# One stream of split weight pieces for the hybrid mixer, with the attention's steps placed between its products

## The chip, the cores and the metric

The kernel runs on one core of one Trainium2 chip. The metric is the device time of one execution in microseconds (us), the median of several runs; lower is better.

## What is computed

The reference is a pair of transformer blocks on 512 tokens of 1024 channels, all in f32. The change touches the middle part of the first block, the hybrid mixer, between two feed-forward parts (`ffn1`, `ffn2`):

```
h = h + 0.5 * rms_norm(swiglu(rms_norm(h, g1)), g2)          # ffn1
u = rms_norm(h, mix_pre_g)
gate_br, x_br, q, k, v, g_lru, g_attn = split(u @ w_in)       # widths 1024 1024 1024 256 256 1024 1024
xc = causal_depthwise_conv(x_br)                              # 4 taps
r, i = sigmoid(block_diag(xc, w_a)), sigmoid(block_diag(xc, w_x))
log_a = -8 * r * softplus(-lambda);  a = exp(log_a)
b = sqrt(max(-expm1(2 * log_a), 0)) * (i * xc)
y_lru = scan(a, b) * gelu(gate_br)                            # h[t] = a[t] h[t-1] + b[t]
y_attn = sliding_window_attention(rope(q), rope(k), v, sinks) # 16 heads of 64, 4 kv heads, window 128
m = (sigmoid(g_lru) * (y_lru @ w_proj_lru) + sigmoid(g_attn) * (y_attn @ w_proj_attn)) @ w_out
h = h + rms_norm(m, mix_post_g)
h = h + 0.5 * rms_norm(swiglu(rms_norm(h, g3)), g4)          # ffn2
```

The second block (an even mixer, a window attention with context, and two layers of a mixture of 32 experts) is not touched.

## The kernel before

Activations lie transposed: 128 channels on the partitions, 512 tokens along the row, eight such tiles (`KT` = 8) to 1024 channels. A weight matrix comes from HBM in chunks of 1 MB (two output tiles) into `slot0` and `slot1` in turn, issued by SyncE in `stream` (L409 to L417); a slot is loaded again once the second tile made from it is done (`full[1]`, `full[3]`).

**Split products.** Where precision allows TensorE's faster f32r form, a product is made of three: weight and activation are each cut into a high part (a copy rounded to f32r) and a low part (what is left). For each of the eight k, high weight x low activation and high x high; then eight times low weight x high activation: 24 matmuls of 512 columns for an output tile (`split_products`, L527 to L543). Half a slot, the weights of one output tile, is a *piece*. ScalarE makes the high part of a piece (`high`, L1089), another engine the low part: VectorE in the feed-forwards (`low`, L1477), GpSimd in the mixer (`low`, L2070). Semaphores `wh_ready`, `wl_ready` and `wh_used` order them. Elsewhere (`dense`, L525) a tile is eight plain f32 matmuls, each of which shows as two rows in the trace. Four PSUM banks take the tiles in turn, with `full[j]` and `free[j]`.

**Queues.** Every engine works through its own list strictly in order, written out by hand. Nothing is planned at run time.

**The junction** between two parts (`junction`, L1056 on ScalarE and L1479 on VectorE): per k, the last part's output is scaled by its norm factor and added to `lat`, and the sum times the gain is split; TensorE starts the next part's first tiles k by k. The norm factor `rs` itself comes later, from a sum of squares on TensorE, a square root on ScalarE (L1068) and a reciprocal on VectorE (L1470). In the feed-forwards three tiles are opened this way (`gate_up`), in the mixer two.

**The mixer** was a chain of stages:
- `xbr` and `q1`, 16 split tiles; VectorE scales each by `rs`, makes the normalised u1 (L1877) and the convolution (L1879, L1882).
- the LRU's block-diagonal products (L901, L902), per tile two f32 matmuls and two sigmoids on ScalarE (L1287, L1288), one behind the other.
- `kv1`, plain f32 on u1, with `partner` (L908, a matmul with a permutation for rope); Exp and Tanh on ScalarE (L1292, L1293); on VectorE, 1 - a^2 by way of a reciprocal (L1895 to L1900), and rope (L1642 to L1645).
- `gate`, plain f32; Sqrt and Gelu (L1307, L1310), scans (L1909), the gated product (L1914).
- a phase end: all engines wait for one another (L344).
- `attend`: 32 units (a pair of heads and 128 queries). Per unit: scores (L692), mask and maximum (L1608, L1614), exponentials (L1171), transposes (L710), their copies (L1182), products with the values (L727), normalisation (L1633), a turn (L735) and its copy (L1191). GpSimd copies the queries (L2026). Unit m's steps stand beside those of units m-1 to m-4. Then a second phase end.
- splits of u1, LRU output and attention output (L1921, L1923, L2118), then `merge`, 32 split tiles in rounds of four (gate, projection, gate, projection), with Sigmoid on ScalarE (L1332) and L1929 and L1931 on VectorE.
- `out1`, plain f32, with `output` (L1045, L1046) and the sum of squares (L638, L640).

The core of a split tile and of the merge order:

```python
for k in range(n):
    for part_of, flag in ((high, first and k == 0), (low, False)):
        mm = nc.tensor.matmul(out, piece[0][k], part_of[k], start=flag, stop=False)
mm.then_inc(wh_used, 1)
low_ready()
for k in range(n):
    mm = nc.tensor.matmul(out, piece[1][k], high[k], start=False, stop=(last and k == n - 1))
```

Of the kernel before, what the change touches and what calls it, by code (L numbers as in the profile page):

```python
# [50 lines left out]
MERGE_PIECES = 4 * KT  # L51

PIECES_BEFORE, _n = {}, 0
for _name, _pieces in ((1, FFN_PIECES), ("mixer", 2 * KT), ("merge", MERGE_PIECES), (2, FFN_PIECES), ("even_in", 2 * KT),
                       ("even_out", KT), ("qkv", KT + 4)):
    PIECES_BEFORE[_name] = _n
    _n += _pieces
# [17 lines left out]
DENSE = [("gu1", 22, 11), ("down1", 8, 2), ("xbr", 4, 2), ("q1", 4, 2), ("kv1", 2, 1),  # L75
         ("gate", 4, 2), ("merge", 16, 8), ("out1", 4, 2), ("gu2", 22, 11), ("down2", 8, 2),
# [37 lines left out]
def program(nc, d):  # L114
    ctx = ExitStack()
    with ctx:
# [10 lines left out]
        with ExitStack() as plain:  # L127
# [6 lines left out]
            big = shared("big", BIG)  # L134
        w_low = [sb(f"w_low{s}", [P, SLOT], F32R) for s in range(2)]
# [6 lines left out]
        sb("big_rest", [P, BIG - 2 * FT * S])  # L142
        cxt = cxt_s[:, :].rearrange("p (k t) -> p k t", k=KT)
# [9 lines left out]
        tabs = sb("tabs", [P, 4, S])  # L153
# [34 lines left out]
        xbr = part(0, [KT, XPAD])  # L188
        xc = part(KT * XPAD, [KT, S])
        o = KT * (XPAD + S)  # L190
        gr = part(o, [KT, S])
        gi = part(o + KT * S, [KT, S])
        qt1 = part(o + 2 * KT * S, [KT, S])
        kt1 = part(o + 3 * KT * S, [2, S])
        qk1 = part(o + 2 * KT * S, [KT + 2, S])
        v1 = part(o + 3 * KT * S + 2 * S, [LT, C])
# [7 lines left out]
        lru_low = split_view(KT * XPAD)  # L204
        u1_low, att_low = u_high, u_low
        u1_high, lru_high, att_high = split_view(0), split_view(o + KT * S), split_view(o + 2 * KT * S)

        p1_high = split_view(o + KT * S)
        p1_low = [flat[a // (FT * S)][:, a % (FT * S):a % (FT * S) + S] for a in
                  [o + k * S for k in range(5)] + [FT * S + k * S for k in range(2)] + [o + 3 * KT * S]]  # L210
        assert o + 5 * S <= FT * S and FT * S + 2 * S <= o + KT * S
        lru_w = ar_u[:, KT * S:KT * S + 2 * KT * P].rearrange("p (g k c) -> p g k c", g=2, k=KT)
        merged = gr
# [75 lines left out]
        bank = [ctx.enter_context(nc.psum_tensor(f"bank{i}", [P, 512], F32)) for i in range(8)]  # L289
# [219 lines left out]
        def _(pe):  # L509
# [45 lines left out]
            def gate_up(n, J):  # L555
# [5 lines left out]
                def piece(j):  # L561
                    s, at, ring = ffn_piece(j)
                    return tiles_of(hi_ring[ring], KT), tiles_of(w_low[s][:, at], KT)
# [1723 lines left out]
```

## Time and profile before

| | us |
|---|---|
| median of 3 runs | 3428.01 (3425.63 to 3429.47) |
| the profiled execution | 3430.5 |
| its span, first to last instruction | 3428.7 |
| TensorE matmul busy | 2938.1 (86%) |
| VectorE busy | 1341.5 (39%) |
| ScalarE busy | 794.0 (23%) |
| GpSimd busy | 513.7 (15%) |
| HBM traffic | 203 GB/s over the span |
| mean granted TensorE clock | 0.907 of full speed |

In the profile PE is TensorE's matmuls, PEld its weight loads, DVE VectorE, ACT ScalarE, POOL GpSimd, SP SyncE. A number like L811 is a line of the kernel. Matmul rows overlap, since their ends are modelled: the spacing of their starts is the rate. PEclk is the granted clock, 1.0 for 2.4 GHz and 0.5 for 1.2 GHz. The mixer lies between about 404 and 1025 us of the span.

### The profile page before, as it was taken

To read this page: it belongs to the slowest core of one execution; us is meant where nothing else is said; L and a number is where in the kernel's file an instruction comes from. 1 tells how busy PE (TensorE), PEld (TensorE's weight loads), DVE (VectorE), ACT (ScalarE), POOL (GpSimd) and SP (SyncE) were. 2 spreads that over 40 slices of the span, in tenths; PEclk is the share of its full clock that TensorE was granted. 3 is DMA by queue.
4 is the path that set the end of the run, shared out by engine and by line. 5 is a ranking of instruction groups with operands and counts; after the bars stand their busy time and mean duration, and the time that the engine had idled before them with its cause. 6 is when DMAs were issued, how large, how long until landed. Compare 5 with 4: busy or idle time off the path is not lost. (4 is left out here: it accounts for less than half of the span.)

```text
span 3428.7 us, 37322 instructions
## 1 busy us (share of the span) xinstructions
PE 2938.1 (86%) x12832; PEld 1906.0 (56%) x12832; DVE 1341.5 (39%) x2369; ACT 794.0 (23%) x1393; POOL 513.7 (15%) x604
## 2 busy tenths in 40 slices
PE   6999888898998999699876888887587986888886
PEld 4888664476856888477653333333365843333333
DVE  4776575664117675612231111111458822111112
ACT  3332323343313322222220000000325711000000
POOL 0111140005400011131301111111310000111110
PEclk9999999758999999899977999998698997999997
DMA  4666421101223566411026999999010024999997
GB/s 162 220 220 220 155 98 50 37 0 63 97 103 137 196 214 236 152 50 49 25 94 238 400 400 403 397 401 358 29 62 1 0 100 175 404 402 396 402 401 291
DMA packets 117463, 671.63 MB, mean 196 GB/s; under 512 B 16398, under 2 KB 20878, under 8 KB 51984
## 3 DMA queue, kind: packets, MB, share of 16 engines
q1 hardware_dynamic: 77456, 542.37, 40.6%
q0 software_dynamic: 33600, 104.90, 8.7%
q10 hardware_dynamic: 6336, 23.50, 1.8%
q8 instruction: 35, 0.57, 0.1%
q14 instruction: 36, 0.29, 0.0%
HBM read 672.52 MB, written 24.38 MB: 203 GB/s over the span
## 5 line engine op out<-in xcount | busy, mean ns | idle before, releaser
L811 PE MATMUL bank<-big 128*64 128x512 f32 x1040 | 482.8, 609 | 105.5 <-DMA big<-in_w 103.8
L814 PE MATMUL bank<-big 128*64 128x512 f32 x1040 | 485.0, 611 | 0.0
L1792 DVE TENSOR_TENSOR big<-big,bank 64x512 f32<-64x512 f32 x65 | 44.9, 692 | 919.0 <-ACT big L1229 919.0
L811 PEld LDWEIGHTS bank<-big 128*64 128x64 f32 x1040 | 139.0, 140 | 418.6 <-issue 416.5
L826 PE MATMUL bank<-big 128*64 128x512 f32 x1040 | 288.8, 707 | 44.4 <-DVE big L1796 44.4
L1524 DVE SCALAR_TENSOR_TENSOR tabs<-tabs,tmp 128x1024 f32<-128x1024 f32 x160 | 193.2, 1222 | 175.3 <-DMA tabs<-in_wm 174.4
L537 PE MATMUL bank<-act_low 128*128 128x512 f32 (+1 forms) x480 | 166.1, 363 | 47.9 <-POOL u_split L2081 25.5
L2096 POOL DMA_DIRECT2D tabs<-in_wm x160 | 84.8, 530 | 743.2 <-DVE tabs L1524 742.4
L826 PEld LDWEIGHTS bank<-big 128*64 128x64 f32 x1040 | 83.4, 160 | 201.1 <-issue 199.7
L537 PE MATMUL bank<-u_split,w_high 128*128 128x512 f32 x448 | 179.1, 400 | 8.2 <-ACT w_high L1089 8.2
L537 PE MATMUL bank<-act_high,w_high 128*128 128x512 f32 x438 | 175.7, 401 | 10.8 <-POOL u_split L2118 10.8
L537 PE MATMUL bank<-act_low,w_high 128*128 128x512 f32 x458 | 170.1, 396 | 9.5 <-POOL w_low L2070 8.4
L1089 ACT ACTIVATE w_high<-slot 128x1024 fp32r<-128x1024 f32 (+1 forms) x116 | 117.7, 1040 | 232.5 <-DMA slot<-in_w 123.2
L543 PE MATMUL bank<-u_split,w_low 128*128 128x512 f32 x656 | 162.2, 389 | 3.0 <-DVE w_low L1477 3.0
L1229 ACT ACTIVATE big<-bank 64x512 f32<-64x512 f32 x65 | 38.2, 588 | 537.5 <-PE bank L811 537.5
L537 PE MATMUL bank<-u_low,w_high 128*128 128x512 f32 x384 | 151.6, 395 | 0.0
L2070 POOL TENSOR_TENSOR w_low<-slot,w_high 128x1024 fp32r<-128x1024 f32 x48 | 117.3, 2447 | 221.5 <-ACT w_high L1089 221.5
L543 PE MATMUL bank<-act_high,w_low 128*128 128x512 f32 (+1 forms) x608 | 146.2, 382 | 0.0
L1235 ACT ACTIVATE big<-bank 128x512 f32<-128x512 f32 x65 | 38.8, 597 | 461.9 <-PE bank L826 461.9
L543 PEld LDWEIGHTS bank<-u_split,w_low 128*128 128x128 f32 x656 | 123.0, 188 | 29.3 <-DVE w_low L1477 3.8
L814 PEld LDWEIGHTS bank<-big 128*64 128x64 f32 x1040 | 138.8, 140 | 0.0
L543 PE MATMUL bank<-act_low,w_low 128*128 128x512 f32 (+1 forms) x592 | 135.5, 372 | 0.0
(339 smaller groups left out, 5408.4 us busy)
## 6 DMA issues: line engine op xcount, KB each, us to landing
big<-in_w SPq DMA_DIRECT2D x402, 1024.0 KB
slot<-in_w SPq DMA_DIRECT2D x100, 1024.0 KB, 4.8
tabs<-in_wm POOLq DMA_DIRECT2D x160, 512.0 KB, 4.8
slot<-in_wd SPq DMA_DIRECT2D x16, 1408.0 KB, 6.8
big<-yb ACTq DMA_DIRECT2D x20, 512.0 KB, 4.8
rows<-big ACTq DMA_DIRECT2D x10, 512.0 KB, 2.6
lat<-in_x SPq DMA_DIRECT2D x1, 2048.0 KB, 9.5
out<-lat SPq DMA_DIRECT2D x4, 512.0 KB, 3.2
```

Source lines behind the costliest of these rows:

```text
L537: mm = nc.tensor.matmul(out, piece[0][k], part_of[k], start=flag, stop=False)
L543: mm = nc.tensor.matmul(out, piece[1][k], high[k], start=False, stop=(last and k == n - 1))
L811: ga = nc.tensor.matmul(bank[0][lo, :], xT[:, 4 * c + k, :], wslot[c][:, k * EF:(k + 1) * EF], **flags)
L814: mm = nc.tensor.matmul(bank[0][hi, :], xT[:, 4 * c + k, :], wslot[2 + c][:, k * EF:(k + 1) * EF], **flags)
L826: mm = nc.tensor.matmul(bank[4][half, :], hT[:, 2 * c + k, :], wslot[4 + c][:, k * D + n * 512:k * D + (n + 1) * 512], start=(c == 0 and k ...
L1089: nc.scalar.activation(rings[ring][:, 0:at.stop - at.start], slot[s][:, at], ACT.Copy).then_inc(wh_ready, 1)
L1229: nc.scalar.activation(hsil[MB:2 * MB, :], bank[0][0:MB, :], ACT.Silu).then_inc(q["sg_ready"], 1)
L1235: nc.scalar.activation(ysb, bank[4][:, :], ACT.Copy).then_inc(q["y_ready"], 1)
L1524: nc.vector.scalar_tensor_tensor(mslot[m % 2], mslot[m % 2], 1.0, crow, ALU.mult, ALU.mult, accum_out=modf[:, idx:idx + 1]).then_inc(mod_d ...
L1792: nc.vector.tensor_tensor(hmul[MB:2 * MB, :], hsil[MB:2 * MB, :], bank[0][MB:2 * MB, :], ALU.mult).then_inc(q["h_ready"], 1)
L2070: nc.gpsimd.tensor_tensor(w_low[s][:, at], slot[s][:, at], rings[ring][:, 0:at.stop - at.start].bitcast(F32), ALU.subtract).then_inc(wl_re ...
L2096: pool.dma_start(mslot[m % 2], d["wm"][(MOD_OF[1] + MOD_OF[2])[m] // 2]).then_inc(mod_load[m % 2], 16)
```

## The change

The mixer becomes one stream of 68 pieces (34 chunks, the same weights in another order): tiles 0 to 7 x branch, 8 to 15 q, 16 and 17 k, 18 and 19 v (256 columns wide), 20 to 27 attention gate, 28 to 35 LRU gate (Gelu), 36 to 43 gate of the LRU projection, 44 to 51 LRU projection, 52 to 59 attention projection, 60 to 67 output. All 68 are split products. The phase ends inside the mixer are gone.

- All gates and projections of u use the unnormalised u split at the junction (`u_high`, `u_low`); the norm factor goes on the products (`scaled`), into the rope tables, and for the values, whose tokens lie on the partitions, into `rs_col`, made by four narrow matmuls. u1 and its split are gone.
- The opening is the feed-forwards': three tiles are opened k by k.
- The low halves of the weights are made by VectorE (`mixer_low`), none by GpSimd.
- The attention's 108 steps (36 x 3 kinds) are spread over tiles 22 to 50, at six hooks in each tile, every four matmuls. Score banks 2 and 3 are read by one VectorE instruction, the sink rides along as one more column, and the output overwrites the queries. In that stretch the products use banks 0 and 1 alone.
- Sigmoid of a gate is (tanh(x/2) + 1)/2. The LRU's 1 - a^2 is (a^2 + 1) times a Tanh, with no reciprocal. Its constants are made at the end of ffn1 (`lru_constants`).
- GpSimd's first loads of modulation tiles for ffn2 wait for tile 51.

The diff, cut to its core:

```diff
-DENSE = [... ("xbr", 4, 2), ("q1", 4, 2), ("kv1", 2, 1),
-         ("gate", 4, 2), ("merge", 16, 8), ("out1", 4, 2), ...
+XBR, QT, KV, VT, GA, GATE, GL, PL, PA, OUT1 = 0, 8, 16, 18, 20, 28, 36, 44, 52, 60
+MIXER_PIECES = OUT1 + KT
+FIRST_ATT, LAST_ATT, HOOKS = 22, 50, 6
+DENSE = [... ("mixer", MIXER_PIECES // 2, MIXER_PIECES // 4), ...
...
+        def att_steps(t, hook=None):
+            n = (LAST_ATT - FIRST_ATT + 1) * HOOKS
+            at = [divmod(z * n // ATT_STEPS, HOOKS) for z in range(ATT_STEPS)]
+            return [z for z, (tile, h) in enumerate(at) if tile + FIRST_ATT == t and hook in (None, h)]
...
         @block.tensor
+            def att1(z):
+                U, kind = divmod(z, 3)
+                if kind == 0 and U < 4 * KT:
+                    pe.wait_ge(s_evac, U + 2)
...
+                elif kind == 1 and 0 <= U - 2 < 4 * KT:
+                    pe.wait_ge(exp_ready, u + 1)
+                    pe.wait_ge(t_evac, u + 1)
...
+            def mixer_free(t):
+                held = t - 4 if t < GA + 2 or t >= OUT1 + 2 else t - 2
+                pe.wait_ge(free[held % 4], done(held))
...
+            def mixer_tile(t, lo, hi, ready=None):
+                pe.wait_ge(wh_ready, W_MIX + t + 1)
+                mixer_free(t)
+                for n in range(2 * KT):
+                    if n % 4 == 0:
+                        for z in att_steps(t, n // 4):
+                            att1(z)
+                    mm = nc.tensor.matmul(out, wh[n // 2], (lo, hi)[n % 2][n // 2], start=(n == 0), stop=False)
+                mm.then_inc(wh_used, 1)
+                pe.wait_ge(wl_ready, W_MIX + t + 1)
+                for k in range(KT):
+                    if k % 4 == 0:
+                        for z in att_steps(t, 4 + k // 4):
+                            att1(z)
+                    mm = nc.tensor.matmul(out, wl[k], hi[k], start=False, stop=(k == KT - 1))
+                mm.then_inc(full[t % 4], 1)
...
+            opening(1, R_MIX, W_MIX, mixer_piece)
+            for t in range(3, MIXER_PIECES):
...
+                if t == 4:
+                    for n in range(LT):
+                        mm = nc.tensor.matmul(bank[7][:, 2 * n:2 * n + 2], rs[:, n * P:(n + 1) * P], ident[:, 0:2], start=True, stop=True)
+                if 5 <= t < 5 + KT:
+                    lru_products(t - 5)
+                if QT + 1 <= t < QT + 1 + KT + 2:
+                    partner(t - QT - 1)
...
         @block.scalar
+            def mixer_high(p):
+                s, at = piece_at(p)
+                used = p - 3 if p < 6 else p - 1
+                high(s, at, ring_of(p), 16 * (plan["mixer"][1] + p // 4 + 1), W_MIX + used, hi_ring, lows=True)
...
+            for p in range(2, OUT1):
+                if QT < p <= QT + KT + 2:
+                    raw(p - QT - 1)
+                if p in (VT + 1, VT + 2):
+                    values(p - 1)
...
+                if 6 <= p < 6 + KT:
+                    lru_gates(p - 6)
+                if p == 14:
+                    act.drain()
+                    decays(0, 4)
+                if p == 15:
+                    decays(4, KT)
+                if p == 17:
+                    roots()
+                for z in att_steps(p):
+                    att1(z)
+                if GA + 2 <= p < GA + 2 + KT:
+                    tanh_half(p - 2, xbr[:, p - 2 - GA, 0:S])
+                if p in (GATE + 5, GATE + 9):
+                    gelus(p - GATE - 5)
...
+                mixer_high(p + 2)
...
         @block.vector
                 r0 = plan[f"gu{n}"][0]
-                dve.wait_ge(wl_ready, PIECES_BEFORE[n])
-                low(n, 0)
-                low(n, 1)
+                if n == 1:
+                    low(n, 0)
+                    low(n, 1)
...
+                if n == 1:
+                    lru_constants()
+                    for p in range(2):
+                        mixer_low(p)
                 rsqrt(S)
...
+            for p in range(1, OUT1 + 1):
+                t = p - 1
+                if t < QT:
+                    scaled(t, xbr[:, t, CONV1 - 1:XPAD])
...
+                if 4 <= p + 1 and p + 1 not in (GA, GA - 1):
+                    mixer_low(p + 1)
+                if t < QT:
+                    conv(t)
...
+                if QT + 2 <= p < QT + 2 + KT + 2 - 1:
+                    rotate(p - QT - 2)
+                if p in (15, 17):
+                    for n in range(4):
+                        powers(2 * (p - 15) + n)
+                if p == VT - 1:
+                    mixer_low(p + 2)
+                if p == VT:
+                    scans(0)
+                    scans(2)
+                if p == VT + 1:
+                    rotate(KT + 1)
+                    scans(4)
+                    scans(6)
+                    mixer_low(p + 1)
+                for z in att_steps(p):
+                    att1(z)
...
+            for q in range(2):
+                low(2, q)
             rsqrt(S)
...
         @block.gpsimd
             mod_loads(1)
-            ...
+            pool.wait_ge(full[(PA - 1) % 4], done(PA - 1))
             mod_loads(2)
```

`mixer_low` is one VectorE subtraction of 1024 elements a row, as L1477. `rotate` is the old rope step (L1642 to L1645). On ScalarE the new `decays` is an Exp, a Tanh and a Square per tile, on VectorE the new `powers` one operation per tile.

## Rows read from the trace of the kernel before

**Rows 1.** By stretch: busy us (rows) of PE, PEld, DVE, ACT, POOL; clock; DMA; GB/s.
```profile
431.00:521.30 90.30, 80.75 (x338) 64.07 (x337) 66.18 (x85) 18.09 (x18) 35.25 (x14) 0.96 0.25 92
521.30:546.80 25.50, 15.37 (x33) 5.50 (x32) 0.69 (x1) 8.85 (x14) 0.00 (x0) 1.00 0.11 41
546.80:576.90 30.10, 30.10 (x103) 19.35 (x102) 24.52 (x24) 14.91 (x22) 0.00 (x0) 1.00 0.11 36
576.90:641.00 64.10, 61.42 (x143) 26.73 (x142) 50.32 (x55) 14.88 (x21) 0.00 (x0) 1.00 0.18 66
641.00:794.00 153.00, 131.58 (x521) 97.26 (x522) 107.40 (x346) 68.81 (x237) 28.59 (x43) 0.51 0.02 7
794.00:968.00 174.00, 172.03 (x745) 139.78 (x745) 30.90 (x39) 55.78 (x59) 70.95 (x32) 1.00 0.27 97
968.00:1024.70 56.70, 56.70 (x129) 24.97 (x129) 4.16 (x6) 11.44 (x19) 0.00 (x0) 0.97 0.22 81
```

**Rows 2.** Timeline of both junctions: start, duration (us), engine, line, operation, [idle before].
```profile
409.58 0.68 DVE L1489 TENSOR_TENSOR lat<-lat,ar_f 128x512 f32<-128x512 f32 x1
...
1024.70 0.60 ACT L1048 ACTIVATE ar_u<-bank 128x512 f32<-128x512 f32 x1 [3.80 <-PE bank L525]
...
1030.73 2.36 DVE L1477 TENSOR_TENSOR w_low<-slot,w_high 128x1024 fp32r<-128x1024 f32 x2
...
1034.21 0.68 DVE L1489 TENSOR_TENSOR lat<-lat,ar_f 128x512 f32<-128x512 f32 x1
...
1059.17 0.80 PE L537 MATMUL bank<-u_split 128*128 128x512 f32 x1
...
1060.49 3.35 DVE L1470 RECIPROCAL rs<-rs 128x512 f32<-128x512 f32 x1 [3.62 <-ACT rs L1068]
```

**Rows 3.** Spacing: out1's timeline, L1931's starts (ns, then us), value rows of qkv2.
```profile
1009.48 13.04 PE L525 MATMUL bank<-big,slot 128*128 128x512 f32 x30
...
L1931 DVE TENSOR_TENSOR big<-tmp x8: 693/1340/1343, 811.8 to 966.7; 128x512 f32 x8
...
2556.24 0.28 PE L998 MATMUL bank<-act_low 128*128 128x256 f32 x1
...
2556.59 0.28 PE L998 MATMUL bank<-act_low 128*128 128x256 f32 x1
```

**Rows 4.** The second attention: timeline of TensorE, and a stretch as in rows 1.
```profile
2655.41 1.04 PE L710 MATMUL bank<-consts,big 128*128 128x128 f32 x8
...
2657.13 0.60 PE L697 MATMUL bank<-big 64*128 64x256 f32 x4
2657.66 2.00 PE L727 MATMUL bank<-big 128*128 128x64 f32 x16
...
2640.00:2680.00 40.00, 38.81 (x312) 32.61 (x313) 34.92 (x103) 28.00 (x75) 2.31 (x8) 1.00 0.00 1
```

**Rows 5.** VectorE: one timeline row, two lines' durations (ns min/median/max), first and last start.
```profile
437.04 2.34 DVE L1860 TENSOR_TENSOR lam<-lam 128x8 f32<-128x8 f32 x1
...
L1882 DVE SCALAR_TENSOR_TENSOR big<-big,vecs x24: 750/752/2971, 449.9 to 497.4; 128x512 f32<-128x512 f32 x24
...
L1909 DVE TENSOR_TENSOR_SCAN big<-big x8: 1224/1225/1225, 609.4 to 622.6; 128x512 f32<-128x512 f32 x8
```

**Rows 6.** Timeline of ffn2's first stall on TensorE.
```profile
1069.31 0.79 PE L537 MATMUL bank<-u_split,w_high 128*128 128x512 f32 x1 [4.09 <-ACT w_high L1089]
1069.90 0.63 PE L537 MATMUL bank<-u_low,w_high 128*128 128x512 f32 x1
```

**Rows 7.** ScalarE: two lines' durations and starts; groups of instructions (busy, mean ns).
```profile
L1292 ACT ACTIVATE big<-big,lam x8: 722/722/724, 549.7 to 559.7; 128x512 f32<-128x512 f32 x8
...
L1293 ACT ACTIVATE big<-big,lam x8: 705/706/708, 550.3 to 560.3; 128x512 f32<-128x512 f32 x8
...
L1307 ACT ACT_TABLE_LOAD x2 | 2.6, 1283 | 0.4 <-issue 0.4
```

**Rows 8.** The page, DMA issues: KB each, us from issue to landing.
```profile
slot<-in_w SPq DMA_DIRECT2D x100, 1024.0 KB, 4.8
```

More of the change, by code:

```diff
@@ L73 @@
 MOD_ROUND = {1: [5] * 11, 2: [5] * MOD_SWITCH + [0] + [5] * (10 - MOD_SWITCH)}
-DENSE = [("gu1", 22, 11), ("down1", 8, 2), ("xbr", 4, 2), ("q1", 4, 2), ("kv1", 2, 1),
-         ("gate", 4, 2), ("merge", 16, 8), ("out1", 4, 2), ("gu2", 22, 11), ("down2", 8, 2),
+DENSE = [("gu1", 22, 11), ("down1", 8, 2), ("mixer", MIXER_PIECES // 2, MIXER_PIECES // 4),
+         ("gu2", 22, 11), ("down2", 8, 2),
          ("even_in", 8, 8), ("even_out", 4, 4), ("q2", 4, 2), ("kv2", 2, 2), ("wo", 4, 2)]
@@ L486, in _ @@
             stream_down("down1")
-            stream("xbr", 2)
-            stream("q1", 2)
-            stream("kv1", 1)
-            stream("gate", 2)
-            stream("merge", 8)
-            stream("out1", 2)
+            stream("mixer", MIXER_PIECES // 4)
             stream("gu2", 11)
@@ new lines, in raw, with values @@
+            def raw(x):
+                act.wait_ge(full[x % 4], done(QT + x))
+                nc.scalar.activation(qk1[:, x, :], bank[x % 4][:, :], ACT.Copy).then_inc(free[x % 4], 1)
+            def values(t):
+                if t == VT:
+                    act.wait_ge(rcol_ready, 1)
+                act.wait_ge(full[t % 4], done(t))
+                for at in range(2):
+                    n = 2 * (t - VT) + at
+                    x = nc.scalar.activation(v1[:, n, :], bank[t % 4][:, at * C:(at + 1) * C], ACT.Copy, scale=rs_col[:, n:n + 1])
+                x.then_inc(free[t % 4], 1)
@@ L1867, in _ @@
[L1867 to L1877 removed]
+            ffn(1, 0, "ffn1_pre_g")
@@ new lines, in _, with scaled @@
+            junction(1, vec("mix_pre_g"), lambda k: u_high[:, k, :], lambda k: u_low[:, k, :], (vh_ready, KT), v_ready)
+            for p in (2, 3):
+                mixer_low(p)
+            nc.vector.memset(xbr[:, :, 0:CONV1 - 1], 0.0)
+            rsqrt(S)
+            cw, cb = vec("conv_w"), vec("conv_b")
+            def scaled(t, dst):
+                dve.wait_ge(full[t % 4], done(t))
+                nc.vector.tensor_tensor(dst, bank[t % 2 if t >= GA else t % 4][:, :], rs[:, 0:S], ALU.mult).then_inc(free[t % 4], 1)
@@ L1878, in _, with conv @@
+            def conv(t):
                 dve.drain()
@@ new lines, in merged_split, with by_gate @@
+            def merged_split(t):
+                dve.wait_ge(mh_ready, 2 * KT + t + 1)
+                nc.vector.scalar_tensor_tensor(m_low[:, t, :], tmp[:, t % 4, :], 0.5, m_high[:, t, :].bitcast(F32), ALU.mult,
+                                               ALU.subtract).then_inc(mx_ready, 1)
+            def by_gate(t, gate, dst):
+                dve.wait_ge(full[t % 4], done(t))
+                nc.vector.scalar_tensor_tensor(dst, gate, 1.0, bank[t % 2][:, :], ALU.add, ALU.mult).then_inc(free[t % 4], 1)
@@ L2153, in tiles @@
     return t.transpose(0, 2, 1, 3).reshape(n // 2, P, CHUNK)
-def mixed(*ws):
-    n = ws[0].shape[1] // P
-    return tiles(np.stack([w.reshape(D, n, P) for w in ws], 2).reshape(D, -1))
 def moving(w):
```

680 lines of the change are left out of this document (394 added, 286 removed).

## The prediction

> **What bounds the kernel now.** I read the busy times by stage first, then where tile 3 of a feed-forward starts after a junction, then the spacing of TensorE's rows, and last the rows of VectorE and ScalarE that the new order loads. The rest of the kernel is untouched, so only the stretch from the end of ffn1's sum (404 us) to the last product of out1 (ScalarE reads it at 1024.70 [rows 2]) counts. In it TensorE works almost alone on weights at a full clock in xbr/q1, kv1, gate, merge and out1 [rows 1]: these are TensorE-bound. Two stages are not. The LRU products (521 to 547 us) keep it 15.4 of 25.5 us busy, waiting for ScalarE's two sigmoids per tile. The attention and what follows it (641 to 794 us) show a granted clock of 0.51, the 1.2 GHz level, with next to no DMA: 153 us for work that the engine does at 2.4 GHz elsewhere, between phase ends at which all engines wait. DMA carries under 100 GB/s in every stage of the mixer [rows 1], so no transfer bounds it.
>
> **What TensorE does after the change.** It issues one stream of 68 pieces. The prices per row at 2.4 GHz are starts against starts. A plain f32 tile is 16 rows; 30 rows took 13.04 us, the last one's 0.59 of duration among it, so 0.43 us each, 6.9 us a tile. A split tile is 24 rows; four tiles of merge took (966.7 - 811.8)/7 = 22.1 us, 5.53 a tile, waits included [rows 3]. I take 5.5. A 256-wide row of a value tile comes every 0.12 us (three rows in 0.35) [rows 3].
> 1. The new opening is the feed-forward's, with three pieces instead of two. In ffn2 the first addition to lat stands at 1034.21 and tile 3 starts at 1059.17, 24.96 us later; here that addition is at 409.58 [rows 2], so tile 3 starts at 434.5.
> 2. Tiles 3 to 67 without the two value tiles: 63 x 5.5 = 346.5 us. Value tiles: 2 x 48 x 0.12 = 11.5.
> 3. LRU products: 8 x 4 f32 rows x 0.43 = 13.8. Rope partners: 10 x 2 x 0.43 = 8.6. The transposition of the factor: 8 narrow rows, 1 us.
> 4. Attention, 32 units, at the spacing of the second attention, which ran at clock 1.00 [rows 4]: transposes 8 rows in 1.04, the last one's 0.28 among it (0.11 to 0.12), score rows 4 in 0.53 (0.13; from 2657.13 to 2657.66), products with values about 0.12. A unit with two key tiles has 4 + 4 + 8 + 1 rows, 2.0 us; one of the 8 with a single key tile 1.3; together 24 x 2.0 + 8 x 1.3 = 58. I add 7 for some 100 changes between kinds of work: 65 us.
> These give 434.5 + 346.5 + 11.5 + 13.8 + 8.6 + 1 + 65 = 881.
>
> **What is late next.** VectorE gets all low halves (GpSimd did them), ScalarE the highs as before, and both queues are in order. GpSimd goes silent, which helps VectorE: one 8-element operation took 2.34 us beside a GpSimd subtraction, and the convolution's step 2.97 at worst against 0.75 as a median [rows 5]. So I price at the medians.
> - Tile 4. The reciprocal of the norm is ready at 1060.49 + 3.35 - 624.63 = 439.2 [rows 2]. VectorE then has, ahead of low(4): three scalings (0.6 each) and two convolutions (four steps of at most 0.75 [rows 5], 3.1), 8 us, and low(4) itself, 1.2 (two took 2.36 [rows 2]): ready 448.7. Tile 4 starts when bank 0 is free (440.0) and has its high part done at 443.8: 4.9 us of idle. A stall of 4.1 us in ffn2 was followed by rows 0.43 us apart [rows 6]; I add 3 us for the clock after this one. Low(5) then comes at 453.6, ahead of need, and with 5.0 to 5.6 us per tile against TensorE's 5.5 + 1.7 VectorE keeps up.
> - Steps 14 to 17 of ScalarE. An Exp, a Tanh and a Square per tile, 0.6 us apart (a Tanh starts at 550.3 behind an Exp at 549.7 [rows 7]), plus a table load of 1.28 [rows 7] make step 14 10.4 us and step 15 9.1, against tiles of 6.4. High(17) comes 1.2 us late; then eight roots with their table make high(19) come about 3.3 us late, and value tile 18 needs it after 8 rows. 4.5 us.
> - Tile 20. Low(20) stands behind eight scans (1.22 each [rows 5]) with their multiplications (0.6), 15 us, two rope steps of 2.1, and a late low(19): ready about 10 us after tile 20 starts, its high part takes 3.7: 6.2 us idle and again 3 for the clock.
> - Tiles 22 to 50. Each takes 5.5 + 65/29 = 7.7 us on TensorE. The old stage (641 to 794), splits included, cost VectorE 107.4/32 = 3.4 and ScalarE 68.8/32 = 2.2 us per unit [rows 1], both upper bounds. At 1.1 to 1.24 units per tile VectorE has 4.2 + 0.6 + 1.2 = 6.0, ScalarE 2.7 + 1.06 + 0.6 = 4.4. Both fit. The two rounds of four Gelus bring two table loads each (1.28 [rows 7]) and 2.4 us, and a copy of probabilities behind them is wanted one unit later: 4 us twice, 8 in all.
> - Tile 60 waits for merged(7), which takes about 3.5 us after tile 59 against 3.2 us of earlier k: 0.5.
> Sum of stalls: 7.9 + 4.5 + 9.2 + 8 + 0.5 = 30. The last product ends at 911, against 1024.7: 113.7 gained. VectorE's two lows ahead of the junction to ffn2, 2.36 us [rows 2], now stand before the reciprocal, in idle time: 116.
>
> **What costs nothing.** The constants of the LRU (27 small operations, 0.25 apart, 7 us) and lows 0 and 1 (2.4) move to VectorE's idle time before the reciprocal at ffn1's end; ScalarE's Exp there adds a table load of 1.28 at the start of down1, which could cost 0 to 1.3 us. Dropping the LRU's reciprocals, u1, and the copies around attention takes work off VectorE that no longer ends a stage. SP's loads keep their rule: a slot is asked for once its second tile is done and wanted two tiles later, 11 us or more, and 1 MB lands in 4.8 [rows 8]. ScalarE issues the LRU weights, also 1 MB, at step 4 behind a wait for tile 3's high part, two tiles ahead of their use; what queues behind it is high(6), not yet due. GpSimd's two early loads of modulation now wait for tile 51 and are wanted in ffn2 only.
>
> The profiled execution took 3430.5 us with a span of 3428.7; 3430.5 - 116 = 3314.5. The median of the runs is 2.5 below the profiled one, so I predict **3312 us**.
>
> Here the spacing matters most. The Trainium skill (TensorE: Matmul & The Clock Gate, section "Wait — 56ns, not 53.3ns?") has 512-column matmuls start 215.7 ns apart, which makes a tile 5.18 us and the sum 20 us less, 3292; as an estimate from that page it stands aside, since these tiles were measured at 5.53.
>
> **The rivals.**
> - *No new stalls* (0.20). The bursts of VectorE and ScalarE are overlapped better than my step-by-step count: 30 us less, 3282. For it: ffn2 loses little to such waits. Against it: the order of low(4) and low(20) is fixed in the code.
> - *A wait per unit* (0.20). Every unit crosses TensorE, VectorE and ScalarE three times, and each step is placed at a fixed row. If a step comes 1 us early once per unit, 32 us more: 3344. For it: in the old attention TensorE waits on VectorE and ScalarE.
> - *The clock falls between the steps* (0.05). If in the mixed tiles (160 + 65 = 225 us) the lower level held half of the time, they would take 225/0.75 = 300, 75 us more: 3387. Against it: 2640 to 2680 ran at 1.00 with attention rows alone [rows 4]; for it: 641 to 794 did not [rows 1]. The Trainium skill (same page, "A second HAM failure mode: psum-queue depth-cycling") says that small idle gaps between groups of matmuls can make the clock swing; by that rule this is what the hooks would do.
> - *The three engines take turns* (0.04), the case on the slower side. It happens if TensorE's wait for the scores' bank pair or for the transposed probabilities comes before VectorE's step has begun, so that a unit costs its engines' sum: 2.0 + 3.4 + 2.2 = 7.6 us, 32 x 7.6 = 243 instead of 65: 178 more, 3490. It decides from 4.0 us lost per tile (116/29).
> - My forecast, 0.51.
>
> **The numbers.** A measurement of this kernel tells 0.2% (7 us) from no change. Faster by more than that: 0.95; within it 0.01; slower 0.04. Unknown costs: spacing 5.45 to 5.6 per tile is -3 to +6; attention's rows 58 to 90, the upper end being 2.8 us per unit; stalls 10 to 50. Range 3284 to 3350.
>
> **What would show it.** Right: granted clock about 1.0 from 440 to 900 us; no stage with clock 0.5; last out1 product near 911; VectorE's low the releaser at tiles 4 and 20, ScalarE's high at 18; the mixed tiles 7.5 to 8 us each; GpSimd empty in the mixer. Wrong: tiles 22 to 50 above 9 us, the clock at 0.5 there, or waits for an engine in all tiles.

## The result and the profile after

The changed kernel takes 3309.36 us (median of 4 runs, 3304.0 to 3313.84), the kernel before 3428.74 in the runs beside it: a ratio of 0.9653, 95% interval 0.9637 to 0.967. The profiled execution took 3313.84 us with a span of 3311.8, so the span fell by 116.9 us. The prediction said 3312 for the median and 3314.5 for the profiled run, in a range of 3284 to 3350.

The page after, its first rows:

```profile
span 3311.8 us, 36836 instructions
PE 2852.1 (86%) x13016; PEld 1892.8 (57%) x13016; DVE 1327.2 (40%) x2265; ACT 812.7 (25%) x1402; POOL 375.2 (11%) x516
...
POOL 0111000000000111322101111110400001111110
PEclk9999999999989999899869999997779997999988
```

GpSimd is silent between the feed-forwards. The stretches of the new mixer, by granted clock (columns as in [rows 1]):

```profile
438.60:448.60 10.00, 6.79 (x30) 5.28 (x29) 9.29 (x13) 0.60 (x1) 0.00 (x0) 1.00 0.59 211
448.60:458.90 10.30, 9.11 (x26) 7.52 (x26) 9.66 (x14) 1.06 (x1) 0.00 (x0) 0.50 0.00 0
458.90:574.90 116.00, 107.58 (x468) 81.07 (x466) 74.68 (x99) 55.26 (x80) 0.00 (x0) 1.00 0.21 73
574.90:581.70 6.80, 5.75 (x14) 4.49 (x15) 3.96 (x4) 1.06 (x1) 0.00 (x0) 0.50 0.00 0
581.70:912.80 331.10, 325.95 (x1624) 256.20 (x1622) 167.87 (x294) 151.73 (x313) 1.04 (x2) 1.00 0.23 82
```

TensorE is filled to over nine tenths, the 153 us at the 1.2 GHz level [rows 1] are gone, and the lower level is left in two places, 10.3 and 6.8 us long. What TensorE waits for between 425 and 920 us (line of the waiting row, releaser; us in total, times, longest):

```profile
PE bank L992 <- DVE w_low L1730: 10.4, 2, 6.0
PE bank L603 <- DVE u_low L1685: 9.0, 3, 8.4
PE bank L1026 <- DVE big L2113: 2.9, 1, 2.9
PE bank L1004 <- ACT w_high L1201: 0.4, 1, 0.4
```

L603 is the opening of a feed-forward, as before. The two waits in L992 (the low rows of a tile) are those of tiles 4 and 20, the one in L1026 (a rope partner) falls in tile 16. None is in the attention's lines 930, 940, 953 or 961. Below, high(p) and low(p) are the making of the two halves of piece p. The first wait, in VectorE's timeline (L2085 and L2088 are a convolution, L1730 a low half):

```profile
437.04 3.35 DVE L1660 RECIPROCAL rs<-rs 128x512 f32<-128x512 f32 x1 [3.58 <-ACT rs L1180]
440.47 0.69 DVE L2081 TENSOR_TENSOR big<-bank,rs 128x512 f32<-128x512 f32 x1
441.25 0.55 DVE L2085 TENSOR_SCALAR big<-big,vecs 128x512 f32<-128x512 f32 x1
441.88 2.41 DVE L2088 SCALAR_TENSOR_TENSOR big<-big,vecs 128x512 f32<-128x512 f32 x3
...
445.60 2.40 DVE L2088 SCALAR_TENSOR_TENSOR big<-big,vecs 128x512 f32<-128x512 f32 x3
447.92 0.69 DVE L2081 TENSOR_TENSOR big<-bank,rs 128x512 f32<-128x512 f32 x1
448.52 1.21 DVE L1730 TENSOR_TENSOR w_low<-slot,w_high 128x1024 fp32r<-128x1024 f32 x1
```

and what it does to TensorE, and again at tile 20 (its timeline):

```profile
449.79 2.93 PE L992 MATMUL bank<-u_split,w_low 128*128 128x512 f32 x6 [4.40 <-DVE w_low L1730]
...
575.95 2.50 PE L992 MATMUL bank<-u_split,w_low 128*128 128x512 f32 x5 [6.00 <-DVE w_low L1730]
```

Six rows in 2.93 us, behind the first stall, are 0.45 us apart; at the full clock they stand 0.23 apart. The brackets, 4.40 and 6.00 us, count from the modelled end of the last row. Between TensorE's weight loads, of which one stands before each row, the pauses are 4.8 and 6.4 us, and 3.3 at the partner in tile 16; these figures are used below. VectorE starts the low half of tile 20 at 574.67, behind the eighth scan, and with its end TensorE goes on.

Where a tile begins (its first high row, L985) and how long it is until the next one, worked out from those rows in several kernels:

```
tile                           3      4      5    6-8   9-12  13-15    16  17-19    20     21   22-50      52-59  61-66
changed, start             435.7  441.6  454.9                      536.5  545.9  566.0  579.5  586.6
changed, profile after      5.89  13.33   8.72   7.21   8.04   6.33   9.44  20.13  13.50   7.02   7.76 mean   5.44   5.60
reordered                   5.89   6.26   6.86   7.5*   8.04   6.34   7.58  19.48   5.57   5.95   7.76        5.44   5.60
low halves moved alone      5.88   6.26   6.86   7.5*   8.04   6.34   9.97  20.50   5.57   6.03   7.76        5.44   5.60
no attention                5.89  13.68   8.48   7.21   8.04   6.34   9.44  20.49  13.49   6.25   5.48        5.44   5.60
attention rows twice        5.89  13.33   8.70   7.21   8.04   6.34   9.42  20.14  13.48   7.24   9.45        5.44   5.60
(* 8.1 for tile 6, 7.2 for 7 and 8)
```

The last low row of out1 starts at 905.5; ScalarE reads the bank at 905.94, where it stood at 1024.70 [rows 2].

### The profile page after: what moved, and what is told of

Its sections match the earlier page's. It is cut to its first block and busy times, and to the rows that moved or that the text cites. A ratio compares the mean times of both kernels' runs of the same rounds, so it can differ in the third digit from the quotient of the medians.

```text
span 3311.8 us, 36836 instructions
## 1 busy us (share of the span) xinstructions
PE 2852.1 (86%) x13016; PEld 1892.8 (57%) x13016; DVE 1327.2 (40%) x2265; ACT 812.7 (25%) x1402; POOL 375.2 (11%) x516
## 5 line engine op out<-in xcount | busy, mean ns | idle before, releaser
L852 PE MATMUL bank<-big 128*64 128x512 f32 x1040 | 486.7, 613 | 110.1 <-DMA big<-in_w 108.3
L852 PEld LDWEIGHTS bank<-big 128*64 128x64 f32 x1040 | 139.4, 141 | 426.2 <-issue 424.0
L573 PE MATMUL bank<-act_low 128*128 128x512 f32 (+1 forms) x480 | 166.8, 364 | 47.9 <-POOL u_split L2382 25.5
L1201 ACT ACTIVATE w_high<-slot 128x1024 fp32r<-128x1024 f32 (+1 forms) x134 | 136.8, 1041 | 226.7 <-DMA slot<-in_w 89.1
L579 PE MATMUL bank<-u_split,w_low 128*128 128x512 f32 x656 | 163.7, 392 | 3.1 <-DVE w_low L1667 3.1
L985 PE MATMUL bank<-u_split,w_high 128*128 128x512 f32 x400 | 158.9, 397 | 0.0
L985 PE MATMUL bank<-u_low,w_high 128*128 128x512 f32 x368 | 155.5, 423 | 0.2 <-ACT w_high L1201 0.2
L579 PEld LDWEIGHTS bank<-u_split,w_low 128*128 128x128 f32 x656 | 123.8, 189 | 29.6 <-DVE w_low L1667 4.0
L573 PE MATMUL bank<-u_split,w_high 128*128 128x512 f32 x320 | 128.0, 400 | 8.2 <-ACT w_high L1201 8.2
L573 PEld LDWEIGHTS bank<-act_low 128*128 128x128 f32 x480 | 93.9, 196 | 70.0 <-issue 24.3
L573 PE MATMUL bank<-u_split 128*128 128x512 f32 x336 | 131.6, 392 | 0.0
L573 PE MATMUL bank<-u_low,u_split 128*128 128x512 f32 x336 | 130.7, 389 | 0.0
L573 PE MATMUL bank<-u_low,w_high 128*128 128x512 f32 x320 | 127.3, 398 | 0.0
## 6 DMA issues: line engine op xcount, KB each, us to landing
lat<-in_x SPq DMA_DIRECT2D x1, 2048.0 KB, 10.3
```

The costliest lines, as they stand in the source:

```text
L852: ga = nc.tensor.matmul(bank[0][lo, :], xT[:, 4 * c + k, :], wslot[c][:, k * EF:(k + 1) * EF], **flags)
L985: mm = nc.tensor.matmul(out, wh[n // 2], (lo, hi)[n % 2][n // 2], start=(n == 0), stop=False)
L1201: nc.scalar.activation(rings[ring][:, 0:at.stop - at.start], slot[s][:, at], ACT.Copy).then_inc(wh_ready, 1)
```

## The experiments

All numbers are medians beside 7 to 9 runs of the kernel before (3430.11, 3431.71 and 3430.09 in the three groups). Line numbers in a fence are those of the kernel it shows.

### The changed kernel again

> The changed kernel itself, as the base of this group: 3309 us, ratio 0.965 to the kernel before. Nothing is told apart here; the other runs of the group are read against it.

3307.96 us (3307.7 to 3308.82), ratio 0.9644 [0.9629, 0.9659]. It is the base of all that follows; tile for tile it repeats the table within 0.6 us.

### The order of VectorE and ScalarE mended

```diff
-                if 4 <= p + 1 and p + 1 not in (GA, GA - 1):
+                if p in (1, 2):
+                    mixer_low(p + 3)
+                if 6 <= p + 1 and p + 1 not in (GA, GA - 1):
                     mixer_low(p + 1)
...
                     rotate(KT + 1)
+                    mixer_low(p + 1)
                     scans(4)
+                if p == VT + 2:
                     scans(6)
-                    mixer_low(p + 1)
...
                 if p == 15:
+                    mixer_high(p + 2)
                     decays(4, KT)
                 if p == 17:
-                    roots()
+                    roots(0, 4)
+                    mixer_high(p + 2)
+                    roots(4, KT)
```

> The changed kernel with nothing left out, only VectorE's and ScalarE's queues reordered: low(4) and low(5) ahead of the convolutions, low(20) ahead of scans(4), scans(6) a step later, high(17) ahead of the second set of decays, high(19) between the roots. Theory (the stalls of tiles 4, 16 and 20 are only the place of one operation in an in-order queue): tile 4 falls from 13.3 to 7.2 us, 5 from 8.7 to 7.2, 16 from 9.4 to 6.4, 20 from 13.5 to 6, 21 from 7.0 to 5.6: 20 us less in all, about 3290 us. Rival (VectorE's total work in tiles 3 to 8 and 16 to 21 is the bound, so the wait moves to a later tile): under 7 us less, over 3303 us.

3290.02 us (3285.06 to 3291.44), ratio 0.9586 [0.9572, 0.9599]: 18 us below the changed kernel, with the same computation. TensorE's waits between 425 and 960, and the whole stream by clock:

```profile
PE bank L603 <- DVE u_low L1689: 9.6, 5, 8.4
PE bank L573 <- ACT w_high L1201: 4.1, 1, 4.1
PE bank L579 <- DVE w_low L1671: 1.0, 1, 1.0
PE bank L1026 <- ACT big L1398: 1.0, 1, 1.0
PE bank L992 <- DVE w_low L1734: 0.5, 1, 0.5
...
420.10:894.60 474.50, 467.45 (x2235) 363.61 (x2233) 275.79 (x435) 215.14 (x406) 1.04 (x2) 1.00 0.23 81
```

L573, L579 and most of L603 belong to ffn2. In the mixer both long waits for a low half are gone (0.5 us is left) and the partner waits 1.0 us instead of 2.9; with them went the lower clock: 474.5 us at 1.00 without a break. Tiles 4 to 6 went from 29.3 to 21.2 us, 8.1 less, of which 4.8 had been idle; tiles 20 and 21 from 20.5 to 11.5, 9.0 less with 6.4 idle. So each stall cost its own length and some 3 us more in this execution, of rows at the lower clock.

### VectorE's two moves alone

The first two hunks of the diff above.

> Of the four moves of the reordered kernel only VectorE's two are made: the low halves of pieces 4 and 5 ahead of the first convolutions, the low half of piece 20 ahead of the scans of tiles 4 to 7 (the last two a step later). ScalarE's high halves 17 and 19 stay behind the powers and the roots. Theory: ScalarE's late high(17) and high(19) make VectorE wait in its low halves, and with it the rope step, and so TensorE before a partner: that part (tile 16 at 9.4 us against 7.6, tiles 17 to 19 at 20.1 against 19.5) stays, some 2.5 us, and the time is about 3293 (15 us below the changed kernel's 3308). Rival 1: the high halves were not on the path and the partner waited for VectorE's own queue: 3290, as the reordered kernel. Rival 2: the stalls only wander on, since what the late high halves held back now meets the scans: above 3298.

3294.82 us (3294.18 to 3295.57), ratio 0.9606 [0.9593, 0.9619]: 13 us below the changed kernel, 5 above the reordered one. The theory holds (3293), though its part is larger than the 2.5 us it gave. What stayed is this wait, which in the reordered kernel is down to 1.0 us:

```profile
PE bank L1026 <- DVE big L2113: 2.9, 1, 2.9
```

The chain behind it, in the profile of the changed kernel: ScalarE does its Exps, Tanhs and Squares (L1425 is the last) before high(17) (L1201), VectorE waits 3.86 us for that high with its low half, and the rope step queued behind the low half is what the partner needs.

```profile
541.80 0.61 ACT L1425 ACTIVATE tmp<-big 128x512 f32<-128x512 f32 x1
542.32 1.04 ACT L1201 ACTIVATE w_high<-slot 128x1024 fp32r<-128x1024 f32 x1
...
543.39 1.23 DVE L1730 TENSOR_TENSOR w_low<-slot,w_high 128x1024 fp32r<-128x1024 f32 x1 [3.86 <-ACT w_high L1201]
544.54 0.68 DVE L2113 TENSOR_TENSOR big<-bank,tabs 128x512 f32<-128x512 f32 x1
```

The table of TensorE's waits blames VectorE's rope; the engine that was late is ScalarE, one queue further back.

### All low halves on GpSimd

```diff
 def mixer_low(p):
-    s, at = piece_at(p)
-    dve.wait_ge(wh_ready, W_MIX + p + 1)
-    nc.vector.tensor_tensor(w_low[s][:, at], slot[s][:, at], hi_ring[ring_of(p)].bitcast(F32), ALU.subtract).then_inc(wl_ready, 1)
+    return
...
+            for p in range(MIXER_PIECES):
+                s, at = piece_at(p)
+                pool.wait_ge(wh_ready, W_MIX + p + 1)
+                nc.gpsimd.tensor_tensor(w_low[s][:, at], slot[s][:, at], hi_ring[ring_of(p)].bitcast(F32), ALU.subtract).then_inc(wl_ready, 1)
```

> The changed kernel with the mixer's 68 low halves made by GpSimd, as before, and VectorE without them. Theory A (what counts is VectorE's queue; GpSimd at 2.45 us per piece fits in a tile of 5.4): the stalls of tiles 4 and 20 go, VectorE's operations beside a GpSimd one get slower but have slack; 5 to 15 us less, 3295 to 3305. Theory B (GpSimd's reads hold up VectorE's operations with two SBUF inputs, the convolutions to 2.4 us each): tiles 3 to 8 rise from 7.2 to 9 us or more, and 5 to 30 us are lost, 3315 to 3340.

3304.45 us (3301.33 to 3305.04), ratio 0.9634 [0.9619, 0.9649]: only 3.5 us below the changed kernel, in the range of theory A; tiles 5 to 8, at 6.9 to 7.2 us, did not rise to the 9 of theory B. The stalls of tiles 4 (6.26 us now) and 20 (5.57) are gone, so the queue was their cause; but tile 21 takes 10.85 us, tile 22 8.68, and tile 3 begins at 438.7. VectorE became slower beside GpSimd (mixer, groups by line; GpSimd's own subtraction first):

```profile
L2403 POOL TENSOR_TENSOR w_low<-slot,w_high 128x1024 fp32r<-128x1024 f32 x64 | 157.7, 2467 | 317.4 <-ACT w_high L1201 317.4
L2085 DVE SCALAR_TENSOR_TENSOR big<-big,vecs 128x512 f32<-128x512 f32 x24 | 24.1, 1002 | 1.8
L2104 DVE TENSOR_TENSOR_SCAN big<-big 128x512 f32<-128x512 f32 x8 | 15.7, 2001 | 0.3
```

against the changed kernel's

```profile
L2088 DVE SCALAR_TENSOR_TENSOR big<-big,vecs 128x512 f32<-128x512 f32 x24 | 18.0, 752 | 2.1 <-issue 0.4
L2107 DVE TENSOR_TENSOR_SCAN big<-big 128x512 f32<-128x512 f32 x8 | 9.4, 1212 | 0.3
```

### The mended order with the low halves on GpSimd

Both edits together.

> The reordered kernel, with all low halves of the mixer on GpSimd instead of VectorE. Theory: with the order mended, VectorE no longer ends a tile, so taking the subtractions from it frees nothing, and what is left is what GpSimd costs: the opening longer (3 us in the kernel with low halves on GpSimd and the old order) and VectorE's steps stretched beside it: 3291 to 3297, 1 to 7 us above the reordered kernel's 3290. Rival: VectorE's queue still costs something in tiles 4 to 21 and is relieved: 3283 to 3288.

3301.95 us (3299.89 to 3304.84), ratio 0.9625 [0.9612, 0.9638]: 12 us above the reordered kernel, more than the theory's 1 to 7 and far from the rival's gain. Its VectorE timeline at tiles 17 to 21 (L2100 powers, L2105 and L2108 scans, L2117 rope):

```profile
544.69 4.70 DVE L2100 SCALAR_TENSOR_TENSOR big<-tmp,big 128x512 f32<-128x512 f32 x4
...
560.38 2.74 DVE L2117 TENSOR_TENSOR big<-big 128x512 f32<-128x512 f32 x1
563.21 3.32 DVE L2105 TENSOR_TENSOR big<-big 128x512 f32<-128x512 f32 x2
566.60 4.38 DVE L2108 TENSOR_TENSOR_SCAN big<-big 128x512 f32<-128x512 f32 x2
...
574.34 2.34 DVE L2108 TENSOR_TENSOR_SCAN big<-big 128x512 f32<-128x512 f32 x2
576.76 1.29 DVE L2082 TENSOR_TENSOR big<-bank,rs 128x512 f32<-128x512 f32 x2
```

Four powers take 2.50 us alone and 4.70 here, a pair of scans 2.34 and 4.38, one rope addition 0.69 and 2.74. The scans end 9 us later than in the reordered kernel, 3.5 of it since tile 3 begins later (441.1 against 437.6). TensorE's first score rows wait 6.4 us; the profile names no releaser, but they start at 577.55, right behind VectorE's first move out of a bank (576.76, 0.69 long), which stood behind the scans; in the code tile 22 waits for this move, since it takes the bank of tile 20. The change's choice of VectorE for the low halves is worth 12 us once the queue is in order; while it was not, it cost 3.5.

### The LRU's reciprocals put back

```diff
                 dve.wait_ge(decay_ready, t + 1)
+                nc.vector.reciprocal(rope_at, tmp[:, t % 4, :])
+                dve.drain()
                 nc.vector.scalar_tensor_tensor(gr[:, t, :], tmp[:, t % 4, :], 1.0, gr[:, t, :], ALU.add, ALU.mult)
```

Eight reciprocals whose result nobody uses: their time, not their arithmetic.

> The changed kernel with one reciprocal of 128x512 (3.35 us) per LRU tile put back on VectorE in the powers, its result unused: 13.4 us at step 15 and as much at step 17. Theory (VectorE and ScalarE hold each other in steps 14 to 19, so this is added almost whole): 18 to 26 us more, about 3331 us. Rival (VectorE idles enough there): under 5 us more, below 3315.

3335.19 us (3331.53 to 3337.24), ratio 0.9719 [0.9704, 0.9734]: 27 us more, the full price of 8 x 3.35 = 26.8. Put back in the reordered kernel:

> The reordered kernel with the eight reciprocals of 3.35 us put back on VectorE ahead of the powers, which cost 27 us in the old order. Theory: VectorE is the bound of tiles 16 to 19, whatever the order: between 530 and 571 us it idles 3 us in the reordered kernel, so 26.8 less 3, 22 to 28 us more, 3312 to 3318. Rival: the old order made the reciprocals dear, since low(20) stood behind all of them; with it ahead, the merge that needs the scans is far off and 10 to 16 us are enough: 3300 to 3306.

3315.51 us (3313.84 to 3318.65), ratio 0.9665 [0.9652, 0.9678]: 25.5 us above the reordered kernel, as the theory said. Its waits in tiles 16 to 20:

```profile
PE bank L1026 <- ACT big L1398: 12.6, 1, 12.6
PE bank L1010 <- DVE w_low L1734: 10.2, 1, 10.2
```

Each batch of four reciprocals (13.4 us) turns into one wait of TensorE, whatever the order. Without them VectorE idles some 4 us (41.0 less 37.2 busy) between 530 and 571 us of the reordered kernel, so there is nothing for them to hide in.

### The attention in one tile, and in 15

```diff
-FIRST_ATT, LAST_ATT, HOOKS = 22, 50, 6
+FIRST_ATT, LAST_ATT, HOOKS = 22, 22, 6     (and 22, 36, 6 in the other kernel)
```

Both kernels, and the one without attention below, also have one drain more on VectorE per LRU split. It falls in tiles 35 to 40, which take 5.44 us each in the two kernels in which they are bare.

> The changed kernel with all 108 attention steps at the six hooks of tile 22 (18 steps each) instead of tiles 22 to 50; one added drain per LRU split. Theory (the products between the steps cover the latency between the engines and keep the clock up): the steps take 95 to 130 us in place of 65, with the granted clock at 0.5 for much of it; 30 to 65 us more, 3340 to 3375 us. Rival (the gain came from the pieces and the dropped phase ends, and the interleaving itself is worth little): under 10 us more, below 3320.

3345.0 us (3341.64 to 3347.17), ratio 0.9746 [0.9729, 0.9762]: 37 us more, in the theory's range, though the clock fell less than it said. Tile 21 takes 23.9 and tile 22 92.4 us, at this clock:

```profile
579.00:603.00 24.00, 20.88 (x86) 15.12 (x84) 12.11 (x26) 10.26 (x30) 0.00 (x0) 0.64 0.12 44
603.00:695.00 92.00, 80.56 (x462) 61.02 (x461) 47.41 (x138) 50.18 (x167) 0.00 (x0) 0.80 0.00 1
```

and TensorE waits 10.6 us in 13 pieces for ScalarE's copy of an output (L953 <- L1462) and 3.0 us in three for VectorE's reading of the scores. The 32 units cost (23.9 + 92.4) - 2 x 5.44 = 105 us in a block, 66 spread over 29 tiles.

> The changed kernel with the attention's steps in tiles 22 to 36 instead of 22 to 50: half the cover per unit, about 2.3 us of products beside 2.0 us of the unit's own rows. Theory (TensorE is the bound, VectorE and ScalarE have slack): within 4 us of the changed kernel, 3304 to 3312. Rival (each unit brings a wait once its cover is thin, VectorE's steps with the lows and scalings take over): 0.5 us or more per unit, 15 us or more, over 3323.

3313.84 us (3311.05 to 3317.31), ratio 0.9659 [0.9643, 0.9675]: 6 us more, a little outside the theory's 4 and far from the rival's 15. From tile 22 to tile 51 it takes 228.2 us against 225.0, the fuller tiles 10.1 to 10.8 us and one 12.5. How thinly the steps are spread matters little, as long as there are products to put between them; the other 3 us lie outside of these tiles.

### The attention's steps left out

```diff
-            return [z for z, (tile, h) in enumerate(at) if tile + FIRST_ATT == t and hook in (None, h)]
+            return []
```

The attention of the mixer is not computed; semaphores that its steps would have counted are set at the start. The output is that of other data.

> The changed kernel without the first attention's steps on any engine (the rotated queries go on in the place of its output), to price it in the stream. Theory (TensorE's rows and nothing else, no idle): 58 to 66 us less, 3242 to 3250. Rival A (the steps also bring waits): over 75 us less, below 3233. Rival B (part of the rows fell into idle time): under 50 us less, over 3258.

3271.22 us (one run), 37 us below the changed kernel: taken by the time alone the theory fell, and half the price of the attention seemed hidden elsewhere. The tiles say otherwise. Tiles 22 to 50 last 158.8 us instead of 225.0, 66 less, all at 5.44 or 5.6, and ffn2's third tile starts 66 us earlier (871.3 against 937.2). The loss comes 800 us later, in the mixture of experts, which starts at 1644.1 (1708.6) and ends at 2287.1 (2323.6): 643 us instead of 615. (The figures in brackets, and 937.2, are those of the changed kernel's second profile, in which the same tiles take 225.0 us too.) The indirect loads of a stretch around that stage (1600 to 2400 us), of this kernel first and of the changed one:

```profile
L2343 POOL DMA_INDIRECT big<-rows,idx_u x36 | 34.8, 966 | 36.4 <-issue 36.4
```

```profile
L2341 POOL DMA_INDIRECT big<-rows,idx_u x34 | 32.9, 967 | 40.7 <-issue 40.7
```

Other values give another routing. The first products of the stage (L852), 16 rows to a block of tokens, are 560 instead of 528: two more blocks, in a stage that takes 28 us longer. In every kernel that computes the reference there are 34 indirect loads. So the attention costs 66 us of stream; the whole kernel's time was not a measure of it.

### The attention's rows twice

```diff
-                    for s in range(2):
+                    for s in (0, 1, 0, 1):            # scores; products with the values alike
...
-                    for y in range(2 * per):
+                    for y in [*range(2 * per)] * 2:   # transpositions
```

> The changed kernel, in which TensorE issues each score row, each transposition of probabilities and each product with the values twice, to the same place with the same result (the turn of the outputs once). VectorE and ScalarE do what they did. Theory: what the attention costs between the products is TensorE's own rows, at 2.0 us for a unit with two key tiles and 1.3 with one, less the single turn of 0.12: 24 x 1.9 + 8 x 1.2 = 55 more, 3360 to 3368, and the mixed tiles go from 7.8 to 9.7 us. It is also the check on the kernel without attention, whose other data changed more than the attention. Rival 1: a good part of the 66 us of the mixed tiles is waits and changes between kinds of work, which a second copy of the rows does not double: under 40 more, below 3348. Rival 2: the hand-over between engines gets tighter as units take longer on TensorE, and the steps begin to wait: over 65 more, above 3373.

3357.64 us (3356.82 to 3359.46), ratio 0.9787 [0.9772, 0.9802]: 50 us more; tiles 22 to 50 take 274.1 us instead of 225.0, and TensorE waits nowhere in them. That is 5 under the theory's 55, and above the rival's 40. The groups of the doubled rows in the mixed tiles:

```profile
L953 PE MATMUL bank<-big 128*128 128x64 f32 x448 | 53.5, 271 | 0.0
L940 PE MATMUL bank<-consts,big 128*128 128x128 f32 x224 | 29.6, 272 | 0.0
L930 PE MATMUL bank<-big 64*128 64x256 f32 x192 | 27.2, 402 | 0.0
```

So of the 66 us, 49 are these rows; the turn is 32 x 0.12 = 4 by my price; and some 13 are left, by subtraction, for the 100 changes between kinds of work, for which the prediction had 7.

### Unsplit output tiles

```diff
-                    mixer_tile(t, *m_tiles, ...)
+                    plain_tile(t)        # 8 f32 products of 512 columns; m is not split, no low half is made
```

> The changed kernel with tiles 60 to 67 as plain f32 products, as out1 was before, with no low halves made for them. Theory (16 rows of 0.43 us against 24 of 0.23): 6.9 instead of 5.6 us per tile, 8 x 1.3 = 10 us more, about 3319 us. Rival (the making of halves costs the split tiles as much elsewhere): under 3 us more, below 3312.

3320.15 us (3315.99 to 3320.98), ratio 0.9677 [0.9661, 0.9693]: 12 us more, as expected for 8 x (6.9 - 5.5) = 11; in the profiles the eight tiles take 55.1 us instead of 45.1. 24 split rows at 0.23 us are cheaper than 16 at 0.43, and TensorE waits for none of the low halves there: tiles 61 to 66 all take 5.60 us.

## Why the prediction was right

The time came out within 3 us of the forecast, and by the mechanism it named. That it came so near is in part luck: the stalls were 8 us too dear, other terms of the stream 3 us too cheap, and the profiled execution lost some 4 us outside of the mixer. The second group of runs has 3430.11 - 3307.96 = 122 us between the two kernels, where 116 were forecast.

- **The opening.** 434.5 predicted, 435.7 measured. From the first addition to lat (409.81) it is 25.9 us, where ffn2's opening, with three pieces too, took 24.96 [rows 2]. The difference is the clock: the first 13 rows (to 417.76) are the slow ones, most of them 0.43 us apart, against the first 8 in the kernel before.
- **The price of a tile.** 5.5 predicted; bare tiles measured 5.44, those of out1 5.60. The measured price from [rows 3] was right. The rule of the Trainium skill (TensorE: Matmul & The Clock Gate, section "Wait — 56ns, not 53.3ns?"), 215.7 ns from row to row, does not hold for these rows, each with a weight load: 5.44/24 = 0.227 us, at a clock of 1.00.
- **Value tiles, LRU products, partners.** 11.5, 13.8 and 8.6 predicted. Tiles 9 to 12 are 8.04, tiles 13 to 15 6.33, bare ones 5.44: a partner costs 0.89 and a tile's LRU products 1.71, 8.9 and 13.7 us over all. Tiles 17 to 19 of the reordered kernel leave 19.5 - 5.4 - 1.8 = 12.3 for the value tiles.
- **Attention.** 65 predicted, 66 measured (tiles 22 to 50 with and without it), with 49 + 4 of rows instead of 58 and 13 of changes instead of 7.
- **Tile 4.** Idle 4.9 and 3 for the clock predicted, low(4) ready at 448.7. It started at 448.52 and was ready at 449.73, TensorE stood still for 4.8 us, and in all 8.1 us were lost. (The first two rows of [rows 6] start 0.59 us apart; it is the ten behind them that stand 0.43 apart, as the forecast says.)
- **Steps 14 to 17.** 4.5 us predicted at the value tile's high row; TensorE idled 3.3 at a rope partner; the reordered kernel is 5 us below the one that leaves ScalarE's order alone, 3.4 of it in tiles 16 to 19. The late engine was the one named, ScalarE with high(17); the step that failed is who feels it. I followed high(17) straight to TensorE and not into VectorE's queue, where the low half waits for it and holds the rope step.
- **Tile 20.** Idle 6.2 and 3 for the clock predicted; 6.4 idle, and 9.0 in all (tiles 20 and 21 took 20.5, with the mended order 11.5).
- **Gelus.** 8 us predicted, none measured; ScalarE's timeline:

```profile
676.10 0.38 ACT L1483 ACTIVATE big<-bank 128x256 f32<-128x256 f32 x1
676.50 1.28 ACT L1442 ACT_TABLE_LOAD   x1
677.79 2.19 ACT L1442 ACTIVATE big<-big 128x512 f32<-128x512 f32 x4
679.89 1.04 ACT L1201 ACTIVATE w_high<-slot 128x1024 fp32r<-128x1024 f32 x1
680.84 0.25 ACT L1462 ACTIVATE big<-bank 128x128 f32<-128x128 f32 x1
681.11 1.28 ACT L1475 ACT_TABLE_LOAD   x1
684.27 0.51 ACT L1475 ACTIVATE big<-big,small 128x257 f32<-128x257 f32 x1 [1.88 <-DVE small L2169]
```

  The step that failed says "a copy of probabilities behind them is wanted one unit later". The copy (L1483) stands ahead of the Gelus, at 676.10, and behind them and both tables ScalarE waits again, 1.88 us, for VectorE's maxima; in other units it waits 2.87. I had counted ScalarE's sum per tile (4.4 of 7.7 us) without spending what was left on the burst.
- **Tile 60.** 0.5 predicted, 5.89 against 5.44.
- **The sum.** The stalls are 8.1 (tile 4, against the reordered kernel) and, against bare prices, 3.8 (tiles 16 to 19), 9.6 (20 and 21) and 0.5 (60), 22 instead of 30. The terms ahead of them are 3 us over, mostly opening 1.2, value tiles 0.8 and attention 1. The last product came at 905.9 instead of 911.
- **After the stream.** From out1's last read to ffn2's reciprocal 33.9 us (905.94 to 939.84), before 35.8 (1024.70 to 1060.49 [rows 2]): 1.9 for the two low halves, 2.36 predicted. From the reciprocal at ffn1's end (404.94 before, 405.17 after) to ffn2's the change gave 120.9; ffn2, untouched, then took 2.3 us longer (355.1 instead of 352.8), and the rest 1.6. ffn2's share belongs to this execution and not to the change: in the second profile of the same kernel ffn2 took 352.6 us.
- **The dropped reciprocals.** The prediction counts them among the work on VectorE "that no longer ends a stage". Put back they cost 27 us, and 25.5 in the mended order, since VectorE is as good as full in tiles 16 to 19. No term of the sum rested on that sentence.
- **What the parts are worth.** Taken back one at a time, the spreading of the attention is worth 37 us, the dropped reciprocals 27 and the split output tiles 12. The three were not taken back together, and the rest (split products for k, v and the LRU gate, the dropped phase ends, u1) was not separated.

Of the rivals, *no new stalls* (3282) describes what the mended order nearly reached, 3290. *A wait per unit* is refuted: no wait in the attention's lines. *The clock falls between the steps* too: 331 us at 1.00 with all the steps in it, so the rule of the Trainium skill (TensorE: Matmul & The Clock Gate, section "A second HAM failure mode: psum-queue depth-cycling") did not show where products fill the gaps. In one tile, where they don't, the granted clock was 0.80. *The three engines take turns* did not occur.

## What to carry to other kernels

When a stage's work is spread as steps between the products of a dense stream, it costs the stream its rows and little else, here 66 us instead of a stage of 153, splits included. What then matters is the order in the other engines' queues: put what the stream needs next (here the halves of the weights) ahead of anything with slack, and follow a late instruction through the queue of the engine that waits for it. And when part of a computation is left out to price it, read the price in the stretch itself: a stage whose amount of work depends on the data can move by more than what is measured.

## What was not expected of the hardware

- With a stall of 4.8 us on TensorE, up to 449.8, went 10.3 us at the 1.2 GHz level (448.6 to 458.9), with one of 6.4, up to 575.9, 6.8 us (574.9 to 581.7), and with the one at the partner, with VectorE's moves alone, 3.4 us (536.9 to 540.3); with the same wait in the changed kernel went none; the same tiles without the stalls run at 1.00. The length of the slow stretch changes between executions: in the kernel with plain output tiles, which is the changed one up to tile 59, the stall at tile 4 has the same length, 4.4 us by the rows' brackets (up to 449.3), the lower level lasts 6.8 us (446.8 to 453.6), and tiles 4 to 6 take 27.0 us instead of 29.3.
- A GpSimd subtraction of 128x1024 takes 2.47 us, and most of VectorE's operations on SBUF that meet one grow, by about 2 us for each subtraction met: one rope addition 0.69 to 2.74, a pair of scans 2.34 to 4.38. Operations that read a bank did not grow: of 32 moves out of a bank (L2082) in the mixer 11 ran beside a subtraction and took 681 to 692 ns, of 32 readings of the scores (L2167) 19 did and took 685 at most.
- The count of routed blocks is part of the time: two blocks more cost 28 us.
